# Second attention: the bias is added on VectorE in the instruction that takes the minimum

## The chip, the cores and the metric

One core of a Trainium2 chip. The metric is the device time of one execution in microseconds (us).

## The reference

Two blocks run one after the other on 512 tokens of width 2048, in float32. The first is an S5 layer and a gated attention with 16 heads of 128. The second, which matters here, projects its input to an attention part and to an RWKV-7 part, and puts both through one output matrix. Its attention has 16 heads of 64 channels and mixes three dilated windows by the softmax of their log sums:

```
for window, dilation in DIL_PATTERNS:          # (128, 1), (512, 4), (2048, 16)
    o, lse = dilated_window_attention(q, k, v, dilation, window // dilation)
    ...
wts = jax.nn.softmax(jnp.stack(lses), axis=0)
o = jnp.einsum('pbsh,pbshc->bshc', wts, jnp.stack(outs))
```

This equals one softmax over all keys with the logarithm of a count added to each score: the count says how many of the three patterns hold this query and key (no pattern: minus 1e30). The kernel computes it so. Its table `bias` is minus that logarithm. The scores on chip are negated too, so a row's minimum is what the softmax takes off, and the exponential has scale -1.

## The kernel before

Activations lie with channels on the 128 partitions and the 512 tokens along the free axis. A projection is a chain of output tiles of 128 channels. Each weight tile is loaded by SyncE into `wraw`, split into a high part by ScalarE (`make_hi`) and a low part by GpSimd (`make_lo`), and multiplied with three matmuls for each block of 128 input channels (lines 183 to 185). The order on each engine is the order of the code; semaphores tie the engines together.

The second attention comes after the RWKV part of the second block. Two heads make a pair, for they share one tile of 128 channels; there are 8 pairs and 16 heads, written out without a loop. A head has four blocks of 128 queries, b = 3, 2, 1, 0, and a block has (b + 1) * 128 keys, so 512, 384, 256 and 128. For head h the engines do this:

- TensorE, `at_scores`: for each block the product of queries and keys (line 1822), then two more products with the identity that add the table's high and low part (lines 1823 and 1824, "bias products"). Then the 10 transposes of the probabilities of the head before (`at_transpose`, line 1864). After an even head it transposes the pair's values (`at_turn_v`), after an odd head from 3 on it multiplies the probabilities of pair (h - 3) / 2 with the values (`at_values`, line 1897).
- VectorE: ahead of an even head from 4 on `at_gate` (line 1918, the product with the gate); then the four minima (`at_minima`, line 1834), one of the four copies of the transposed probabilities of the head before (`at_copy_dve`, line 1879), and `at_divide`: a reciprocal of two row sums (line 1852) and two products (line 1855), twice.
- ScalarE: the four exponentials with their row sums (`at_exp`, line 1845), the other three copies (`at_copy_act`, line 1888), and the copy of the values after an even head. After an odd head it rounds one output tile to its high part (line 1625).
- GpSimd: for each pair the sum that finishes the rotation of queries and keys (`at_turn`, line 1804), and between two of these the low part of one output tile (`w2_lo`, line 1630).
- SyncE: `at_load` brings queries, keys and values of a pair and the swapped parts (lines 1787 and 1791), `at_load_z` its gate (line 1797). Two sets of buffers serve even and odd pairs. The load of the gate of pair p waits until `at_gate` of pair p - 2 has run, and the load of pair p + 1 stands behind it in SyncE's queue.

A head has three banks of PSUM, by its parity: its scores and later the transposes of its probabilities lie there, so head h waits for the copies of head h - 2. The scores of an even head wait for `at_turn` of their pair.

Of the kernel before, what the change touches and what calls it, by code (L numbers as in the profile page):

```python
# [75 lines left out]
def program(nc, a):  # L76
    ctx = ExitStack()
    with ctx:
# [1553 lines left out]
        def rw_act(act, p, nxt):  # L1632
# [49 lines left out]
            if not nxt:  # L1682
                act.wait_ge(gemm, N_B)
                w2_hi(act, range(0, 3))
                make_hi(act, N_B + 1, 1, (N_B + 1) // 2)
                w2_hi(act, range(3, NBK))
                act.activation(idr, ident[:, :], ACT.Copy)
                act.activation(bhi, xt["bias"], ACT.Copy).then_inc(a_bh, 1)
                for i in (1, 2):
                    act.wait_ge(gemm, N_B + i)  # L1690
                    make_hi(act, N_B + 1 + i, (1 + i) % 2, (N_B + 1 + i) // 2)
# [60 lines left out]

        flat = [r[:, 13:KT, :].rearrange("p k t -> p (k t)") for r in (rhi, rlo)]
        bhi, blo, idr = flat[0][:, 0:1280], flat[1][:, 0:1280], flat[0][:, 1280:1280 + P]
        a_bh, a_bl = sem("a_bh"), sem("a_bl")
        at["p2"] = xt["bias"]

# [24 lines left out]
        def at_load(sp, p):  # L1782
            u = p % 2
            if p >= 2:
                sp.wait_ge(a_s, 6 * (p - 1))
# [20 lines left out]
        def at_scores(pe, h):  # L1806

            p, hd, u = h // 2, h % 2, h // 2 % 2
            if hd == 0:
                pe.wait_ge(a_qk, p + 1)  # L1810
            if h == 0:
                pe.wait_ge(a_bl, 1)
            if h == 1:
                pe.wait_ge(rw_cn, 8)
                pe.wait_ge(rw_sd, 8)
            for b in (3, 2, 1, 0):
                bank, o = as_at[b]
# [19 lines left out]
        def at_exp(act, h):  # L1837
            hd = h % 2
            if h >= 2:
                act.wait_ge(a_pt, 3 * h - 3)  # L1840
            for b in (3, 2, 1, 0):
                bank, o = as_at[b]
                n = (b + 1) * P
                act.wait_ge(a_mx, 4 * h + (4 - b if b >= 2 else 4))
                act.activation(at[f"s{hd}"][:, tri[b]:tri[b] + n], ab_[hd][bank][:, o:o + n], ACT.Exp, scale=-1.0,  # L1845
                               bias=stat(hd, 0, b, b + 1), accum_out=stat(hd, 1, b, b + 1)).then_inc(a_e, 1)
# [21 lines left out]
        def at_part(h, kb):  # L1868
            bank, o = ap_at[kb]
            n = (4 - kb) * P  # L1870
            return at[f"p{h % 3}"][:, p_tri[kb]:p_tri[kb] + n], ab_[h % 2][bank][:, o:o + n]

        def at_copy_dve(d, h):
            if h >= 3:
                d.wait_ge(a_o, (h - 3) // 2 + 1)
            if h == 2:
                d.wait_ge(a_bl, 1)
            d.wait_ge(a_pt, 3 * h + 3)
            d.tensor_copy(*at_part(h, 0)).then_inc(a_pd, 1)

        def at_copy_act(act, h):
            if h >= 3:
                act.wait_ge(a_o, (h - 3) // 2 + 1)
            if h == 2:
                act.wait_ge(a_bl, 1)
            for kb, n in ((2, 1), (3, 2), (1, 2)):
# [3 lines left out]
        def at_values(pe, p):  # L1890
# [4 lines left out]
            for kb in range(4):  # L1895
                for hd in range(2):
                    ins = pe.matmul(banks[1][hs_[hd], kb * P:T],  # L1897
                                    at[f"vt{p % 2}"][:, kb * P + hd * CH:kb * P + (hd + 1) * CH],
                                    at[f"p{(2 * p + hd) % 3}"][:, p_tri[kb]:p_tri[kb] + (4 - kb) * P],
                                    start=(kb == 0), stop=(kb == 3))  # L1900
# [617 lines left out]
```

## Time and profile before

| | |
|---|---|
| time, median of 3 runs | 3248.46 us (3246.85 to 3249.99) |
| profiled execution, first to last instruction (its span; the page has no other time for it) | 3251.0 us |
| mean granted TensorE clock | 0.984 |
| TensorE busy | 3085.9 us, 95% |
| VectorE busy | 1359.9 us, 42% |
| ScalarE busy | 1142.8 us, 35% |
| GpSimd busy | 1645.1 us, 51% |

The second attention runs from about 2946 to 3072 us of the span. In the trace TensorE is PE, VectorE is DVE, ScalarE is ACT, GpSimd is POOL, SyncE is SP; "q" behind an engine is its queue, and an arrow points from what is read to what is written. SBUF tiles appear under the buffer in which they lie (`g`, `wk`, `rhi`), PSUM as `bank`.

### The profile page before, as it was taken

What the parts mean: (1) busy time and instruction counts of PE and PEld (TensorE: products, weight loads), DVE (VectorE), ACT (ScalarE), POOL (GpSimd) and SP (SyncE); (2) the same over time, 40 slices, a digit from 0 to 9 for tenths busy, and PEclk for the clock granted to TensorE, in tenths of its full rate; (3) what the DMA queues carried; (4) which work ended last, traced back from release to release, by engine and by line L of the source; (5) the groups of instructions that cost most, each with busy time, mean ns of one, the idle gap of its engine ahead of it and who ended that gap; (6) DMA issues with size and microseconds to landing.
All of it is one profiled execution on the core that took longest, in us unless ns stands there. A gap on an engine that the chain in (4) does not pass through costs nothing.

```text
span 3251.0 us, 53322 instructions
## 1 busy us (share of the span) xinstructions
PE 3085.9 (95%) x21260; PEld 2411.6 (74%) x21260; DVE 1359.9 (42%) x2058; ACT 1142.8 (35%) x1524; POOL 1645.1 (51%) x1331
## 2 busy tenths in 40 slices
PE   5899989999899999999999989999999999999997
PEld 4677778878678888888877857777777777765676
DVE  8789882120332221231231054345345345345512
ACT  4355553233432232332333242233233233244421
POOL 2555554444677777777754434443443444443242
PEclk9999999999999999999999999999999999999998
DMA  4466665232222222222222332222222222224422
GB/s 152 139 183 174 181 194 178 92 142 95 86 72 94 94 87 94 84 97 89 88 81 78 105 123 100 79 89 86 79 96 82 76 101 81 81 78 121 141 104 90
DMA packets 126977, 348.14 MB, mean 107 GB/s; under 512 B 59873, under 2 KB 62945, under 8 KB 96241
## 3 DMA queue, kind: packets, MB, share of 16 engines
q1 hardware_dynamic: 126832, 346.00, 32.3%
q8 instruction: 118, 1.93, 0.3%
q14 instruction: 27, 0.21, 0.0%
HBM read 306.33 MB, written 34.90 MB: 105 GB/s over the span
## 4 chain that ended last, share of the span: by engine, by line
PE 73%; issue 10%; POOL 8%; DVE 5%; ACT 2%; DMA 0%; POOLq 0%; ACTq 0%; SPq 0%; DVEq 0%
PE bank L183 21%; PE bank L184 20%; PE bank L185 20%; POOL wlo L167 7%; PE bank L1822 1%; PE bank L1150 1%; PE bank L1168 1%; PE bank L1504 1%; ACT whi L162 1%; PE bank L1515 1%; PE bank L1823 1%; PE bank L1897 1%; PE bank L1159 1%; PE bank L1483 0%; PE bank L924 0%
## 5 line engine op out<-in xcount | busy, mean ns | idle before, releaser
L167 POOL TENSOR_TENSOR wlo<-wraw,whi 128x512 fp32r<-128x512 f32 (+1 forms) x916 | 1225.0, 1369 | 1335.3 <-ACT whi L162 1335.3
L183 PE MATMUL bank<-rhi,whi 128*128 128x512 f32 x3648 | 1490.5, 409 | 85.6 <-DVE rlo L770 29.3
L184 PE MATMUL bank<-rlo,whi 128*128 128x512 f32 x3648 | 1431.5, 392 | 0.0
L185 PE MATMUL bank<-rhi,wlo 128*128 128x512 f32 x3648 | 1430.5, 392 | 0.0
L183 PEld LDWEIGHTS bank<-rhi,whi 128*128 128x128 f32 x3648 | 690.7, 189 | 285.8 <-issue 67.3
L184 PEld LDWEIGHTS bank<-rlo,whi 128*128 128x128 f32 x3648 | 691.7, 190 | 147.6 <-issue 15.3
L185 PEld LDWEIGHTS bank<-rhi,wlo 128*128 128x128 f32 x3648 | 690.6, 189 | 147.7
L162 ACT ACTIVATE whi<-wraw 128x2048 fp32r<-128x2048 f32 (+2 forms) x232 | 437.9, 1887 | 546.5 <-PE bank L185 345.6
L978 POOL TENSOR_TENSOR wraw<-wraw,vec 128x512 f32<-128x512 f32 x260 | 266.8, 1057 | 0.0
L882 DVE TENSOR_TENSOR ssum<-ssum,wk 128x512 f32<-128x512 f32 x30 | 21.6, 718 | 315.5 <-ACT wk L872 315.5
L872 ACT ACTIVATE wk<-bank 128x512 f32<-128x512 f32 x32 | 27.9, 872 | 240.2 <-PE bank L185 240.2
L1723 POOL TENSOR_TENSOR g<-g,wk 128x256 f32<-128x256 f32 x80 | 58.7, 756 | 95.1 <-PE bank L1504 64.7
L1388 DVE TENSOR_TENSOR g<-g,bank 128x512 f32<-128x512 f32 x40 | 27.6, 689 | 157.6 <-PE bank L1515 157.6
L1049 DVE SCALAR_TENSOR_TENSOR wk<-bank,rstd 128x512 f32<-128x512 f32 x16 | 11.1, 692 | 180.5 <-PE bank L185 180.5
L1054 DVE TENSOR_TENSOR wk<-bank,rstd 128x512 f32<-128x512 f32 x16 | 11.1, 692 | 168.7 <-PE bank L185 168.7
L1065 ACT ACTIVATE wk<-wk 128x128 f32<-128x128 f32 (+1 forms) x64 | 35.2, 551 | 107.5 <-DVE wk L1026 107.5
L1079 ACT ACTIVATE wk<-bank 128x512 f32<-128x512 f32 (+1 forms) x64 | 22.8, 442 | 130.9 <-PE bank L1159 130.9
L859 DVE TENSOR_TENSOR wk<-wk,g 128x512 f32<-128x512 f32 x16 | 11.1, 692 | 136.5 <-ACT wk L855 136.5
L1047 DVE TENSOR_TENSOR wk<-bank,rstd 128x512 f32<-128x512 f32 x16 | 11.1, 691 | 135.8 <-PE bank L185 135.8
L1021 DVE TENSOR_TENSOR wk<-wk 128x128 f32<-128x128 f32 x64 | 62.5, 1035 | 0.5
L2025 DVE TENSOR_TENSOR g<-g,bank 128x512 f32 (+1 forms) x16 | 11.0, 688 | 121.0 <-PE bank L185 118.6
L1845 ACT ACTIVATE g<-bank,wk 128x512 f32<-128x512 f32 (+1 forms) x64 | 33.4, 525 | 61.0 <-DVE wk L1834 61.0
(364 smaller groups left out, 3015.2 us busy)
## 6 DMA issues: line engine op xcount, KB each, us to landing
wraw<-in_wall_dram SPq DMA_DIRECT2D x224, 1024.0 KB, 4.9
g<-in_bmat_dram SPq DMA_DIRECT2D x16, 512.0 KB, 4.0
g<-scr_e SPq DMA_DIRECT2D x128, 64.0 KB, 3.2
scr_a<-ssum SPq DMA_DIRECT2D x24, 256.0 KB, 2.1
g<-in_xp_dram SPq DMA_DIRECT2D x4, 1024.0 KB, 11.5
g<-in_cmat_dram SPq DMA_DIRECT2D x16, 256.0 KB, 7.1
scr_u<-wk SPq DMA_DIRECT2D x16, 256.0 KB, 2.4
scr_y<-wk SPq DMA_DIRECT2D x16, 256.0 KB, 3.1
```

The lines of the kernel that those rows point to most:

```text
L162: act.activation(whi[:, slot, c], wraw[:, slot, c], ACT.Copy).then_inc(w_hi, 1)
L167: ins = pool.tensor_tensor(wlo[:, slot, c], wraw[:, slot, c], whi[:, slot, c].bitcast(F32), ALU.subtract)
L183: pe.matmul(acc[slot][:, :], whk, rhi[:, k, :], start=(k == first), stop=False)
L184: pe.matmul(acc[slot][:, :], whk, rlo[:, k, :], start=False, stop=False)
L185: ins = pe.matmul(acc[slot][:, :], wlk, rhi[:, k, :], start=False, stop=(k == last))
L978: ins = pool.tensor_tensor(raw[:, k, :], raw[:, k, :], bc(g, 2, [P, KT // QUARTERS, P]), ALU.mult)
L1021: ins = d.tensor_tensor(dg, dg, mask, ALU.add)
L1065: ins = act.activation(sc, sc, ACT.Exp, bias=mf["nm"][:, b:b + 1], accum_out=mf["sum"][:, b:b + 1])
L1150: ins = pe.matmul(banks[bank][:, at:at + w_], mf["qh"][:, b * P:(b + 1) * P], mf["kh"][:, 0:w_], start=True, stop=True)
L1159: ins = pe.transpose(banks[bank][:, at + (qb - kb) * P:at + (qb - kb + 1) * P], mf["s"][:, tri[qb] + kb * P:tri[qb] + (kb + 1) * P], ident ...
L1723: pool.tensor_tensor(ml[hd].rearrange("p (b t) -> p b t", b=NB), ab4[hd][:, :, 0], bc(lv, 1, [P, NB, CH]), ALU.mult).then_inc(rw_ml, 1)
L1845: act.activation(at[f"s{hd}"][:, tri[b]:tri[b] + n], ab_[hd][bank][:, o:o + n], ACT.Exp, scale=-1.0, bias=stat(hd, 0, b, b + 1), accum_out ...
```

## The change

The bias products go, and with them the preparation of the table's two parts: two copies on ScalarE and a subtraction on GpSimd ahead of the stage. The minimum of a block becomes one instruction, `tensor_tensor_reduce`, that reads the scores in PSUM and the table in SBUF, writes their sum to the SBUF buffer of the head's probabilities and its minimum to the statistics. The exponential then reads that SBUF buffer in place of PSUM. Each of the four blocks now signals by itself (`a_s` counts four in a head, not three). The table stays in SBUF throughout; before, its place was taken over by the third of three buffers for transposed probabilities (`p2`), which now lies in two free pieces of SBUF.

```diff
@@ at_scores
-            if h == 0:
-                pe.wait_ge(a_bl, 1)
...
-                pe.matmul(to, at_q[u][hs_[hd], b * P:(b + 1) * P], at_k[u][hs_[hd], 0:n], start=True, stop=False)
-                pe.matmul(to, idr, bhi[:, tri[b]:tri[b] + n], start=False, stop=False)
-                ins = pe.matmul(to, idr, blo[:, tri[b]:tri[b] + n], start=False, stop=True)
-                if b != 1:
-                    ins.then_inc(a_s, 1)
+                pe.matmul(to, at_q[u][hs_[hd], b * P:(b + 1) * P], at_k[u][hs_[hd], 0:n], start=True, stop=True)\
+                  .then_inc(a_s, 1)
@@ at_minima, at_exp
-            for b in (3, 2, 1, 0):
-                bank, o = as_at[b]
-                d.wait_ge(a_s, 3 * h + min(4 - b, 3))
-                d.tensor_reduce(stat(hd, 0, b, b + 1), ab_[hd][bank][:, o:o + (b + 1) * P], AX.X, ALU.min)\
-                 .then_inc(a_mx, 1)
...
+                d.wait_ge(a_pt, 3 * h - 3)
...
+                d.wait_ge(a_s, 4 * h + (4 - b if b >= 2 else 4))
+                d.tensor_tensor_reduce(at[f"s{hd}"][:, tri[b]:tri[b] + n], ab_[hd][bank][:, o:o + n],
+                                       xt["bias"][:, tri[b]:tri[b] + n], 1.0, 3.0e38, ALU.add, ALU.min,
+                                       stat(hd, 0, b, b + 1)).then_inc(a_mx, 1)
...
-                act.activation(at[f"s{hd}"][:, tri[b]:tri[b] + n], ab_[hd][bank][:, o:o + n], ACT.Exp, scale=-1.0,
+                sc = at[f"s{hd}"][:, tri[b]:tri[b] + (b + 1) * P]
+                act.wait_ge(a_mx, 4 * h + 4 - b)
+                act.activation(sc, sc, ACT.Exp, scale=-1.0,
                                bias=stat(hd, 0, b, b + 1), accum_out=stat(hd, 1, b, b + 1)).then_inc(a_e, 1)
@@ at_part
-            return at[f"p{h % 3}"][:, p_tri[kb]:p_tri[kb] + n], ab_[h % 2][bank][:, o:o + n]
+            return at_p(h, kb), ab_[h % 2][bank][:, o:o + (4 - kb) * P]
...
+            if h % 3 == 2:
+                return p2[0] if kb == 0 else p2[1][:, p_tri[kb] - T:p_tri[kb] - T + n]
+            return at[f"p{h % 3}"][:, p_tri[kb]:p_tri[kb] + n]
@@ rw_act, at_pool
-                act.activation(idr, ident[:, :], ACT.Copy)
-                act.activation(bhi, xt["bias"], ACT.Copy).then_inc(a_bh, 1)
...
-            pool.wait_ge(a_bh, 1)
-            pool.tensor_tensor(blo, xt["bias"], bhi.bitcast(F32), ALU.subtract).then_inc(a_bl, 1)
```

On VectorE, at an even head of the middle of the stage, the rows before the change are these (`a_s` is the semaphore of finished scores, `a_pt` of transposes, `a_e` of exponentials):

```order
L1918 TENSOR_TENSOR g<-bank,g 128x512 [waits a_lz1,a_o]
L1834 TENSOR_REDUCE wk<-bank 128x1 [waits a_s] x4
L1879 COPY wk<-bank 128x512 [waits a_pt,a_o]
L1852 RECIPROCAL wk<-wk 128x2 [waits a_e]
L1855 TENSOR_SCALAR g<-g,wk 128x512 [waits vch]
L1855 TENSOR_SCALAR g<-g,wk 128x384
```

and these with the change, at the same place:

```order
L1910 TENSOR_TENSOR g<-bank,g 128x512 [waits a_lz1,a_o]
L1827 ISA g,wk<-bank,wk 128x512 [waits a_s,a_pt]
L1827 ISA wk 128x1
L1827 ISA g,wk<-bank,wk 128x384 [waits a_s]
L1827 ISA wk 128x1
L1827 ISA g,wk<-bank,wk 128x256 [waits a_s]
L1827 ISA wk 128x1
L1827 ISA g,wk<-bank,wk 128x128 [waits a_s]
L1827 ISA wk 128x1
L1873 COPY wk<-bank 128x512 [waits a_pt,a_o]
L1843 RECIPROCAL wk<-wk 128x2 [waits a_e]
```

Four instructions have become eight: behind each one that adds and reduces stands a second that writes one column, the minimum. The order of all else is kept.

On TensorE, at the scores of an odd head, a piece of the difference:

```order
-L1822 MATMUL bank<-wk 128x512
-L1823 MATMUL bank<-rhi 128x512
-L1824 MATMUL bank<-rlo,rhi 128x512
-L1822 MATMUL bank<-wk 128x384
-L1823 MATMUL bank<-rhi 128x384
-L1824 MATMUL bank<-rlo,rhi 128x384
```

and what stands there with the change:

```order
+L1815 MATMUL bank<-wk 128x512
+L1815 MATMUL bank<-wk 128x384
+L1815 MATMUL bank<-wk 128x256
+L1815 MATMUL bank<-wk 128x128
```

Nothing lies between the products of two blocks any more; transposes and value products follow as before.

## Rows read from the trace of the kernel before

**Rows 1.** The page of the profile, its first line

```profile
span 3251.0 us, 53322 instructions
```

**Rows 2.** Busy time by engine in one stretch of the second attention, then clock, DMA share, GB/s

```profile
2960.00:3063.00 103.00, 100.32 (x484) 56.03 (x483) 63.56 (x153) 50.48 (x161) 26.92 (x18) 1.00 0.35 98
```

**Rows 3.** The chain that ended last, five of its pieces (start us, us, what)

```profile
3004.51 1.05 PE bank L1822 x2
...
3016.40 1.12 PE bank L1864 x10
...
3017.52 2.30 PE bank L1897 x16
...
3019.82 1.05 PE bank L1822 x2
...
3065.76 0.43 PE bank L183
```

**Rows 4.** Timeline of head 7 (start us, us, engine, line), TensorE and one VectorE row

```profile
2997.09 0.55 DVE L1855 TENSOR_SCALAR g<-g,wk 128x256 f32<-128x256 f32 x2
...
2997.14 0.50 PE L1823 MATMUL bank<-rhi 128*128 128x512 f32 x1
...
2997.80 0.91 PE L1822 MATMUL bank<-g 64*128 64x384 f32 x2
...
3000.65 0.33 PE L1823 MATMUL bank<-rhi 128*128 128x128 f32 x1
...
3000.93 1.28 PE L1864 MATMUL bank<-ident,g 128*128 128x128 f32 x10
```

**Rows 5.** VectorE groups by form (count | busy us, mean ns | idle before)

```profile
L1834 DVE TENSOR_REDUCE wk<-bank 128x1 f32<-128x512 f32 x16 | 11.1, 691 | 3.6 <-PE bank L1824 3.2
...
L1016 DVE SCALAR_TENSOR_TENSOR wk<-bank,wk 128x512 f32<-128x512 f32 x16 | 11.9, 742 | 0.0
...
L1016 DVE SCALAR_TENSOR_TENSOR wk<-bank,wk 128x128 f32<-128x128 f32 x16 | 5.6, 351 | 27.6 <-PE bank L1150 27.6
...
L1852 DVE RECIPROCAL wk<-wk 128x2 f32<-128x2 f32 x32 | 5.0, 157 | 0.4 <-ACT g L1845 0.4
...
L428 DVE TENSOR_TENSOR_SCAN bank<-g,bank 128x256 f32<-128x256 f32 x16 | 11.1, 695 | 0.6
```

**Rows 6.** Timeline from the end of head 7 on: one pass of the load of a pair

```profile
2998.94 2.00 POOL L1804 TENSOR_TENSOR wk<-wk 128x1024 f32<-128x1024 f32 x1 [8.74 <-DMA wk<-scr_a]
...
3002.25 0.36 ACT L1845 ACTIVATE g<-bank,wk 128x128 f32<-128x128 f32 x1
...
3003.11 0.82 DVE L1855 TENSOR_SCALAR g<-g,wk 128x512 f32<-128x512 f32 x2
...
3004.04 1.56 DVE L1855 TENSOR_SCALAR g<-g,wk 128x256 f32<-128x256 f32 x2
...
3004.12 1.40 POOL L1630 TENSOR_TENSOR rlo<-g,rhi 128x512 fp32r<-128x512 f32 x1 [3.19 <-ACT rhi L1625]
...
3005.52 0.68 DVE L1918 TENSOR_TENSOR g<-bank,g 128x512 f32<-128x512 f32 x1
...
3006.22 0.35 SPq L1797 DMA_DIRECT2D g<-scr_az  x1
...
3006.67 0.39 SPq L1787 DMA_DIRECT2D g<-scr_a  x1
...
3014.09 2.36 POOL L1804 TENSOR_TENSOR g<-g 128x1024 f32<-128x1024 f32 x1 [8.58 <-DMA g<-scr_a]
```

**Rows 7.** ScalarE, one group by form in the second attention

```profile
L1888 ACT ACTIVATE wk<-bank 128x256 f32<-128x256 f32 x10 | 3.8, 382 | 0.0
```

**Rows 8.** Timeline: first minimum of the stage, and SyncE behind the gates of pairs 0 and 5

```profile
2950.87 1.68 DVE L1834 TENSOR_REDUCE wk<-bank 128x1 f32<-128x512 f32 x4
...
2974.65 0.35 SPq L1797 DMA_DIRECT2D g<-scr_az  x1
...
3051.99 0.35 SPq L1797 DMA_DIRECT2D g<-scr_az  x1
```

More of the change, by code:

```diff
@@ L1751, in program @@
                "in1": g2[:, 0:3 * T], "sw1": g2[:, 3 * T:5 * T]}
[L1753 to L1756, printed above, removed]
+        p2 = [w["u"][:, 0:T], wk[:, 5706:5706 + 768]]
         def at_out(p):
@@ L1784, in at_load @@
             if p >= 2:
-                sp.wait_ge(a_s, 6 * (p - 1))
+                sp.wait_ge(a_s, 8 * (p - 1))
                 sp.wait_ge(a_vt, p - 1)
@@ L1821, in at_scores @@
                 to = ab_[hd][bank][:, o:o + n]
-                pe.matmul(to, at_q[u][hs_[hd], b * P:(b + 1) * P], at_k[u][hs_[hd], 0:n], start=True, stop=False)
-                pe.matmul(to, idr, bhi[:, tri[b]:tri[b] + n], start=False, stop=False)
-                ins = pe.matmul(to, idr, blo[:, tri[b]:tri[b] + n], start=False, stop=True)
-                if b != 1:
-                    ins.then_inc(a_s, 1)
+                pe.matmul(to, at_q[u][hs_[hd], b * P:(b + 1) * P], at_k[u][hs_[hd], 0:n], start=True, stop=True)\
+                  .then_inc(a_s, 1)
         def at_minima(d, h):
             hd = h % 2
-            for b in (3, 2, 1, 0):
-                bank, o = as_at[b]
-                d.wait_ge(a_s, 3 * h + min(4 - b, 3))
-                d.tensor_reduce(stat(hd, 0, b, b + 1), ab_[hd][bank][:, o:o + (b + 1) * P], AX.X, ALU.min)\
-                 .then_inc(a_mx, 1)
-        def at_exp(act, h):
-            hd = h % 2
             if h >= 2:
-                act.wait_ge(a_pt, 3 * h - 3)
+                d.wait_ge(a_pt, 3 * h - 3)
             for b in (3, 2, 1, 0):
@@ L1843, in at_exp @@
                 n = (b + 1) * P
-                act.wait_ge(a_mx, 4 * h + (4 - b if b >= 2 else 4))
-                act.activation(at[f"s{hd}"][:, tri[b]:tri[b] + n], ab_[hd][bank][:, o:o + n], ACT.Exp, scale=-1.0,
+                d.wait_ge(a_s, 4 * h + (4 - b if b >= 2 else 4))
+                d.tensor_tensor_reduce(at[f"s{hd}"][:, tri[b]:tri[b] + n], ab_[hd][bank][:, o:o + n],
+                                       xt["bias"][:, tri[b]:tri[b] + n], 1.0, 3.0e38, ALU.add, ALU.min,
+                                       stat(hd, 0, b, b + 1)).then_inc(a_mx, 1)
+        def at_exp(act, h):
+            hd = h % 2
+            for b in (3, 2, 1, 0):
+                sc = at[f"s{hd}"][:, tri[b]:tri[b] + (b + 1) * P]
+                act.wait_ge(a_mx, 4 * h + 4 - b)
+                act.activation(sc, sc, ACT.Exp, scale=-1.0,
                                bias=stat(hd, 0, b, b + 1), accum_out=stat(hd, 1, b, b + 1)).then_inc(a_e, 1)
@@ L1869, in at_part, with at_p @@
             bank, o = ap_at[kb]
+            return at_p(h, kb), ab_[h % 2][bank][:, o:o + (4 - kb) * P]
+        def at_p(h, kb):
             n = (4 - kb) * P
-            return at[f"p{h % 3}"][:, p_tri[kb]:p_tri[kb] + n], ab_[h % 2][bank][:, o:o + n]
+            if h % 3 == 2:
+                return p2[0] if kb == 0 else p2[1][:, p_tri[kb] - T:p_tri[kb] - T + n]
+            return at[f"p{h % 3}"][:, p_tri[kb]:p_tri[kb] + n]
         def at_copy_dve(d, h):
@@ L1875, in at_copy_dve @@
                 d.wait_ge(a_o, (h - 3) // 2 + 1)
-            if h == 2:
-                d.wait_ge(a_bl, 1)
             d.wait_ge(a_pt, 3 * h + 3)
@@ L1883, in at_copy_act @@
                 act.wait_ge(a_o, (h - 3) // 2 + 1)
-            if h == 2:
-                act.wait_ge(a_bl, 1)
             for kb, n in ((2, 1), (3, 2), (1, 2)):
@@ L1898, in at_values @@
                                     at[f"vt{p % 2}"][:, kb * P + hd * CH:kb * P + (hd + 1) * CH],
-                                    at[f"p{(2 * p + hd) % 3}"][:, p_tri[kb]:p_tri[kb] + (4 - kb) * P],
+                                    at_p(2 * p + hd, kb),
                                     start=(kb == 0), stop=(kb == 3))
```

## The prediction

> **What bounds the kernel now.** I read the span first [rows 1]; 3251.0 us is 2.5 us above the median of the runs shown, and since the sum below is a difference inside one trace, I take it off the median. Next come the busy times over the middle of the second attention [rows 2]: TensorE works 100.3 of 103 us at clock 1.00, VectorE 63.6, ScalarE 50.5, GpSimd 26.9. The chain that ended last says the same: a pair's scores start at 3004.51 and the next pair's at 3019.82, so a pair costs 15.31 us, and what lies between is nearly all TensorE [rows 3]. TensorE is the limit today, so what it loses is worth time until the next loop closes. The question is which loop is next and at what length.
>
> **What the change takes from TensorE.** In head 7 the bias products of the widest block lie between 2997.14 and 2997.80, 0.66 us; those of the narrowest between 3000.65 and 3000.93, 0.28 us [rows 4]. The widths go in even steps, so four blocks cost 2 * (0.66 + 0.28) = 1.9 us a head, 3.8 us a pair. TensorE alone would then need 15.3 - 3.8 = 11.5 us a pair, 30 us less over 16 heads. The copies and the subtraction ahead of the stage had no one waiting for them; I count them at nothing. The work that hides them is the last RWKV pair on TensorE. The reciprocal chain on VectorE that lets the first minimum start only at 2950.87 [rows 8] does not depend on them either, so without that cover nothing changes.
>
> **What it adds to VectorE.** No row shows the fused instruction. The nearest is the first attention's, which also reads scores in PSUM and a table in SBUF and writes SBUF: 0.742 us for 512 columns and 0.351 for 128, against 0.691 for today's minimum of 512 [rows 5]. Four blocks: 2 * (0.742 + 0.351) = 2.2 us. The order shows a second instruction behind each; the smallest VectorE row is 0.157 us [rows 5], the lower bound is nothing. I take 0.157, so 2.8 us a head. Upper bound for the main instruction: the scan, 0.695 us for 256 columns where the first attention's form, on the line between its ends, takes 0.48; that is 0.86 ns a column more, 1.1 us for the 1280 columns of a head. A head on VectorE is then 2.8 for the minima, 0.6 for the copy (it takes 0.69, and the next instruction can start a little before its end), and for the divide 0.2 for the first reciprocal, 0.93 from the first two products to the last two, and 0.55 for these [rows 4, 6], about 1.7. Together 5.1 us, and with the gate's 0.68 [rows 6] a pair is 10.9 us. That is below 11.5: by busy time alone VectorE doesn't bind.
>
> **The loop that closes next.** SyncE can't fetch ahead at will: the load of pair p + 1 stands behind the gate's load of pair p, and that waits for `at_gate` of pair p - 2. Rows 6 show one pass. The gate product ends at 3005.52 + 0.68 = 3006.20; the gate's load is issued at 3006.22, the pair's at 3006.67; GpSimd's sum (`at_turn`) starts at 3014.09, so 7.9 us behind the gate's end; it takes 2.36 us, or 2.00 for the other buffers [rows 6], on average 2.2. So 10.1 us behind a gate the next pair's scores can start, and not before. Today that is early: the sum for pair 4 ended at 3000.94 and its scores start at 3004.51 [rows 3, 6], 3.6 us of slack. The slack is less than the 3.8 us that the change takes from a pair, so this load decides.
>
> Where the sum lands matters too. Today it falls on VectorE's minima. Then it would fall on the divide of the odd head, just ahead of the next gate. In rows 6 the last two products of a divide take 1.56 us where a free one has 0.55 [rows 4], and the gate behind them starts at 3005.52, when GpSimd's `w2_lo` (3004.12 + 1.40) ends. So a GpSimd operation holds VectorE's products: 1.0 us here. The Trainium skill says this in "SBUF — State Buffer", section "Who interferes with whom": GpSimd and a VectorE instruction in a two-port mode exclude each other for a whole instruction, while one with a single SBUF input outside of these modes, as the fused one would be, isn't held. By that rule the products would wait for the whole sum and the minima would not; a price list without it gives rival A's time.
>
> With the hold, one pass is: 10.1 from the gate's end to the end of the sum; then the held products, 0.93 + 0.55 = 1.5; `w2_lo` is queued right behind the sum and gets between them, 1.0; the next gate, 0.7; hand-over 0.1. Sum 13.4 us a pair, against 15.3.
>
> **The sum.** Before pair 2's gate load there is a first stretch. It starts with the minimum at 2950.87, bound by VectorE: four heads at 2.8 + 1.7 less about 0.2 of overlap, three copies of 0.6, a gate of 0.7, are 19.7 us, so 2970.6 without any hold. GpSimd works on two weight tiles, one sum and one `w2_lo` in that stretch; laid out in order, these hold the divides for about 4 us, which puts the first gate's end at 2974.6, where it is now (SyncE follows it at 2974.65 [rows 8]). So it gains 0, at best 4. From the gate of pair 0 to that of pair 5 there are five passes: now 3051.99 - 2974.65 = 77.3 us [rows 8], then 5 * 13.4 = 67.0, a gain of 10.3. The last stretch, from the gate of pair 5 to the end of the values of pair 6, is 3065.76 - 3051.99 = 13.8 us now [rows 3, 8]. Then: minima 2.7, the last exponential 0.36 and its hand-over 0.1 [rows 6], the first copy 0.38 [rows 7], scores of head 15 at (1.05 + 3000.93 - 2997.14) - 1.9 = 2.95, transposes 1.12, values 2.30 [rows 3, 4]: 10.0 with the hand-overs, a gain of 3.8. Behind that nothing is changed and all of it moves up. Total 10.3 + 3.8 = 14.1 us: 3248.5 - 14.1 = 3234.4, I say 3234.5.
>
> **Rivals.** A, no hold: VectorE has finished the divide ahead of the sum, or the products don't wait. Then the load loop is 10.1 + 0.7 + 0.2 = 11.0 us and TensorE's 11.5 decides: 5 * (15.5 - 11.5) = 20, and 3.8, and up to 4 in the first stretch: 3221 to 3225. For it: today's sums cost almost nothing. Against it: 1.56 against 0.55 in rows 6. A 0.14.
>
> B, the fused instruction runs at the scan's pace, 1.1 us a head more. VectorE's pair is 10.9 + 2.2 + 1.0 of hold = 14.1, and waits for TensorE come on top; it saves about 6 us: 3242. For it: both keep a running result. Against it: today's minimum keeps one too at 0.691. "Vector Engine (DVE) Microarchitecture Reference" of the Trainium skill, section "Points that are easy to get wrong", halves such instructions when both sources lie in SBUF and aren't bf16; here one is PSUM, so by its letter it wouldn't, but if it did, this rival is what it gives, 3242. B 0.15.
>
> C, slower: the fused instruction and its second one cost over (15.3 - 0.7 - 1.0) / 2 - 2.3 = 4.5 us a head; from there VectorE alone makes a pair longer than 15.3. At twice the scan's excess they cost 5.0 and the stage grows by 8 pairs * 1.0: 3256. An instruction that no row shows leaves room for it. C 0.08.
>
> The forecast, 3229 to 3239, has 0.58; 0.05 is left for effects outside of the stage. TensorE will wait some 2 us in a pair; the clock is 1.00 in rows 2 and might fall at times, but TensorE's own work isn't what ends last then.
>
> **Numbers.** 0.2% is 6.5 us, about what a measurement of this kernel can tell from no change, so the line is at 3242. Faster: forecast, A, half of B, some of the rest, 0.82. Same 0.10, slower 0.08. The range reaches to A's upper part and to B: 3223 to 3243; the likeliest case alone 3229 to 3239.
>
> **What would show it.** Right: the period of pairs is 13.4 us, TensorE waits for GpSimd's sum at even heads, VectorE's products stretch to 2 us beside it. Fused rows near 0.74 and a small second row. The first gate ends at about 2974.6. Wrong: waits on ScalarE or VectorE in place of the sum, a period of 11.5 (A) or 14 (B), or the fused row above 1.2 us.

## The result, and the profile after

The changed kernel takes 3231.28 us, the median of nine runs (3228.34 to 3241.19), against 3248.46 (nine runs, 3235.61 to 3259.39): the ratio is 0.995, with a 95% interval of 0.9938 to 0.9963, so 12 to 20 us less. The forecast was 3234.5, in a range of 3223 to 3243.

The page of the changed kernel, its first line and the busy times (answers [rows 1]):

```profile
span 3239.4 us, 53124 instructions
...
PE 3062.8 (95%) x21132; PEld 2407.9 (74%) x21132; DVE 1350.7 (42%) x2122; ACT 1141.0 (35%) x1522; POOL 1639.7 (51%) x1330
```

The span is 11.6 us shorter than before. This execution was the longest of its nine (3241.19 us), so it is no measure of the whole gain. What repeats is the stage itself. Below, the **stage** runs from the start of the first minimum to the start of the last gate product (pair 7), and a **pass** from the start of one gate product to the next, for the five passes between the gates of pairs 0 and 5. The stage took 121.3 us before and takes 110.1 now, 11.2 less, while the rest of the span is the same to 0.4 us.

Busy time by engine (TensorE, its weight loads, VectorE, ScalarE, GpSimd), then clock, DMA share and GB/s, in the first stretch (to the gate of pair 0) and in the five passes, for the changed kernel:

```profile
2950.43:2975.51 25.08, 20.93 (x71) 13.44 (x70) 15.40 (x60) 15.72 (x46) 8.99 (x8) 0.59 0.34 97
...
2975.51:3040.98 65.47, 56.80 (x286) 36.91 (x287) 49.84 (x156) 36.28 (x120) 17.57 (x10) 0.92 0.43 121
```

and for the kernel before, cut at the same events:

```profile
2950.87:2973.93 23.06, 21.77 (x105) 12.25 (x105) 15.47 (x44) 15.20 (x46) 9.05 (x8) 1.00 0.37 106
...
2973.93:3051.29 77.36, 75.45 (x362) 41.53 (x362) 48.63 (x117) 36.91 (x120) 17.87 (x10) 1.00 0.37 103
```

The first stretch is 2.0 us longer, at a granted clock of 0.59 in place of 1.00. The passes have gone from 77.4 to 65.5 us at clock 0.92. The last stretch, from the gate of pair 5 to that of pair 7, has gone from 20.9 to 19.6 us, at clock 0.83. TensorE is busy 87% of the passes (56.8 of 65.5), before 98%; VectorE 76%, before 63%. Nothing in the row of the passes is full, so waits set part of the pace.

VectorE by form in the changed kernel's second attention (count | busy us, mean ns | idle before), which answers [rows 5]:

```profile
L1846 DVE TENSOR_SCALAR g<-g,wk 128x512 f32<-128x512 f32 x16 | 13.0, 810 | 0.6
...
L1827 DVE CUSTOM_DVE_ANT_0 g<-bank,wk 128x512 f32<-128x512 f32 x16 | 11.0, 687 | 9.0 <-PE bank L1815 9.0
...
L1827 DVE DVE_READ_ACCUMULATOR2_ANT wk<- 128x1 f32 x64 | 5.3, 83 | 0.0
...
L1827 DVE CUSTOM_DVE_ANT_0 g<-bank,wk 128x128 f32<-128x128 f32 x16 | 4.6, 286 | 0.0
```

The fused instruction is the `CUSTOM_DVE_ANT_0`: 687 ns at 512 columns, 286 at 128 (forecast 742 and 351). The instruction behind it, which writes the minimum, takes 83 ns, not 157. The widest product of the divide shows 810 ns, where it had 499 before.

The chain that ended last, six of its pieces in one pass (start us, us, what), answers [rows 3]:

```profile
2976.23 0.35 SPq L1792
...
2978.57 5.45 DMA g<-scr_a
...
2984.09 2.37 POOL g L1799
...
2986.51 1.78 PE bank L1815 x4
...
2988.45 0.28 DVE g L1846
...
2988.73 0.60 DVE g L1910
```

This is the loop of the forecast: gate, load, sum on GpSimd, scores of an even head, held products, gate. (The chain names the scores because VectorE's queue waits for them next; what the gate itself stands behind are the held products.) The same pass in the timeline (start us, us, engine, line), beside a free pair of products for comparison, answers [rows 6]:

```profile
2984.09 2.36 POOL L1799 TENSOR_TENSOR g<-g 128x1024 f32<-128x1024 f32 x1 [12.79 <-DMA g<-scr_a]
...
2984.57 3.51 DVE L1846 TENSOR_SCALAR g<-g,wk 128x512 f32<-128x512 f32 x2
...
2986.41 1.45 POOL L1630 TENSOR_TENSOR rlo<-g,rhi 128x512 fp32r<-128x512 f32 x1
...
2988.65 0.68 DVE L1910 TENSOR_TENSOR g<-bank,g 128x512 f32<-128x512 f32 x1
...
2989.36 0.35 SPq L1792 DMA_DIRECT2D g<-scr_az  x1
...
3009.80 0.81 DVE L1846 TENSOR_SCALAR g<-g,wk 128x512 f32<-128x512 f32 x2
```

From the gate's load (2976.23) to the sum are 7.86 us, forecast 7.9. The sum lasts 2.36. The two products that start beside it take 3.51 us together, where a free pair takes 0.81, and end only behind `w2_lo`. The next gate comes 2.20 us behind the sum's end (forecast 1.5 + 1.0), and the next gate's load at 2989.36, 13.13 us after the last one.

Not every pass is like this one. The windows of this pass and of the fourth:

```profile
2975.51:2988.65 13.14, 12.09 (x63) 7.68 (x64) 11.20 (x32) 7.19 (x24) 3.77 (x2) 1.00 0.41 120
...
3011.24:3027.60 16.36, 13.31 (x57) 8.84 (x58) 9.01 (x33) 7.50 (x24) 5.55 (x3) 0.79 0.33 96
```

The granted clock of the five passes is 1.00, 0.87, 1.00, 0.79 and 1.00. The first and the last, 13.1 and 13.4 us, have the full clock, and in both TensorE waits for the sum and the products are held. They show the loop of the forecast without the clock in it.

### The profile page after: what moved, and what is told of

It reads as the page before. It is cut to its first block, busy times and chain, and to the rows that moved or that the text cites. A ratio compares the mean times of both kernels' runs of the same rounds, so it can differ in the third digit from the quotient of the medians.

```text
span 3239.4 us, 53124 instructions
## 1 busy us (share of the span) xinstructions
PE 3062.8 (95%) x21132; PEld 2407.9 (74%) x21132; DVE 1350.7 (42%) x2122; ACT 1141.0 (35%) x1522; POOL 1639.7 (51%) x1330
## 4 chain that ended last, share of the span: by engine, by line
PE 73%; issue 9%; DVE 7%; POOL 7%; ACT 2%; DMA 1%; SPq 1%; DVEq 0%; POOLq 0%; ACTq 0%
PE bank L183 21%; PE bank L185 20%; PE bank L184 20%; POOL wlo L167 6%; PE bank L1150 1%; PE bank L1168 1%; PE bank L1815 1%; PE bank L1504 1%; ACT whi L162 1%; PE bank L1515 1%; DVE bank L403 1%; DMA g<-scr_a 1%; PE bank L1159 1%; PE bank L1483 0%; PE bank L1855 0%
## 5 line engine op out<-in xcount | busy, mean ns | idle before, releaser
L184 PEld LDWEIGHTS bank<-rlo,whi 128*128 128x128 f32 x3648 | 692.0, 190 | 147.7 <-issue 15.1
L859 DVE TENSOR_TENSOR wk<-wk,g 128x512 f32<-128x512 f32 x16 | 11.5, 717 | 137.1 <-ACT wk L855 131.5
L2028 ACT ACTIVATE wk<-g 128x512 f32 (+1 forms) x16 | 10.1, 632 | 123.5 <-DVE g L2015 123.5
## 6 DMA issues: line engine op xcount, KB each, us to landing
g<-in_xp_dram SPq DMA_DIRECT2D x4, 1024.0 KB, 11.8
```

What stands on the lines that cost most here:

```text
L184: pe.matmul(acc[slot][:, :], whk, rlo[:, k, :], start=False, stop=False)
```

## The experiments

Each kernel's time stands beside the kernel before on the same chip. "First" is the first stretch, and the clock column gives its granted clock and that of the passes.

| kernel | median us (runs); before | ratio, 95% interval | stage | first | the five passes | clock |
|---|---|---|---|---|---|---|
| before | 3248.46 (9) | | 121.3 | 23.1 | 16.3 15.3 15.3 15.3 15.2 | 1.00, 1.00 |
| changed | 3231.28 (9); 3248.46 | 0.9950, 0.9938 to 0.9963 | 110.1 | 25.1 | 13.1 12.7 9.9 16.4 13.4 | 0.59, 0.92 |
| changed, again | 3231.72 (11); 3247.67 | 0.9952, 0.9938 to 0.9965 | 109.5 | 25.1 | 13.1 12.4 10.0 16.2 13.2 | 0.59, 0.92 |
| load ahead | 3225.14 (5); 3253.92 | 0.9913, 0.9897 to 0.9929 | 93.5 | 22.1 | 11.0 11.2 10.5 10.8 11.0 | 0.69, 1.00 |
| load ahead, again | 3219.57 (5); 3247.67 | 0.9917, 0.9899 to 0.9934 | 93.5 | 22.1 | 11.0 11.2 10.6 10.3 11.5 | 0.69, 1.00 |
| low parts late | 3232.59 (6); 3253.92 | 0.9941, 0.9921 to 0.9962 | 108.9 | 22.1 | 10.0 15.0 10.2 16.0 14.8 | 0.69, 0.92 |
| both | 3227.17 (6); 3253.92 | 0.9919, 0.9902 to 0.9937 | 100.3 | 25.1 | 10.5 10.5 11.8 10.2 14.9 | 0.59, 0.97 |
| filled | 3226.21 (5); 3253.92 | 0.9913, 0.9898 to 0.9929 | 103.0 | 22.1 | 13.2 12.7 13.5 12.5 12.6 | 0.69, 1.00 |
| ahead, early fill | 3223.84 (6); 3248.36 | 0.9928, 0.9912 to 0.9943 | 92.5 | 21.2 | 11.5 10.0 11.8 10.2 11.0 | 0.92, 1.00 |
| filled, low parts late | 3231.66 (4); 3248.36 | 0.9944, 0.9924 to 0.9965 | 103.1 | 22.1 | 12.3 11.9 12.4 12.4 15.6 | 0.69, 1.00 |
| idle products | 3248.16 (10); 3248.36 | 1.0005, 0.9991 to 1.0019 | 120.9 | 22.7 | 16.2 15.3 15.3 15.3 15.1 | 1.00, 1.00 |
| before, load ahead | 3249.09 (10); 3248.36 | 1.0004, 0.9991 to 1.0018 | 124.0 | 25.7 | 16.3 15.3 15.3 15.3 15.2 | stage 0.97 |
| filled, low part doubled | 3231.91 (9); 3247.67 | 0.9959, 0.9943 to 0.9975 | 108.7 | 21.7 | 14.6 13.4 14.2 14.0 13.7 | 0.76, 0.93 |
| filled, gate later | 3239.75 (9); 3247.67 | 0.9980, 0.9966 to 0.9995 | 109.8 | 25.8 | 13.8 13.4 14.3 13.6 14.5 | 0.74, 0.94 |

The stage repeats within 0.6 us in the two kernels that were profiled twice; the rest of the span lies anywhere from 3117 to 3130 us, in every kernel. So causes are read from the stage and the passes, and the timed ratio says what is left of them in the end.

**Load ahead** (changed kernel; the load of pair p + 1 no longer stands behind the gate's load of pair p).

```diff
-            for p in range(2, 8):
-                at_load(sp, p)
+            at_load(sp, 2)
+            for p in range(2, 8):
+                if p < 7:
+                    at_load(sp, p + 1)
                 at_load_z(sp, p)
```

> SyncE issues the load of pair p + 1 ahead of the gate's load of pair p, so it no longer waits for a gate. Load theory (load of a pair plus the hold of VectorE make the loop of 13.1 us a pair in the changed kernel): the sum of queries and keys is early again, no even head waits for it, a pair falls to 11.5 us and the time by 5 * 1.6 = 8 us, to about 3223. Clock theory (TensorE at a granted clock of 0.86 is the limit, the load merely arrives in time): no wait on the sum, but a pair stays near 13 us and the time at 3231. VectorE theory (its own work is the limit): also 3231, with VectorE busy without a gap.

> The load-ahead kernel beside the changed one on the same chip. Load theory: 5 to 12 us less than the changed kernel, passes of 11 us and a stage near 94 us, 16 us less than the first profile of the changed kernel. Rival (the first difference came from the chips): the same time as the changed kernel.

A pass goes to 10.9 us on average and the stage to 93.5, 16.6 less than the changed kernel's. In the repeat, on one chip with the changed kernel, the medians are 3219.57 and 3231.72, 12 us apart. TensorE no longer waits for a sum at any even head of the passes, where in the changed kernel it waits 0.54, 3.09 and 0.95 us at three of the five. So the order in SyncE's queue closed the loop. How much of the 11.0 us that the passes lose is the wait itself, and how much the clock, which is 1.00 where it was 0.92, isn't separated; beside the first and the last pass of the changed kernel, which have the full clock too, a pass is 2.1 and 2.3 us shorter. Of the stage's 16.6 us, 3.0 lie in the first stretch, at clock 0.69 in place of 0.59, and other kernels show the same without this edit. In timed difference to the kernel before it is the fastest kernel of the study. This is also the kernel in which the clock is easiest to follow. Its timeline, two rows of TensorE in the first stretch:

```profile
2941.35 2.43 PE L1855 MATMUL bank<-ident,g 128*128 128x128 f32 x10 [2.64 <-DVE g L1846]
...
2945.29 4.60 PE L1815 MATMUL bank<-g 64*128 64x512 f32 x8 [1.51 <-ACT g L1880]
```

and its windows, 8 us from about the second row on and then the five passes:

```profile
2946.00:2954.00 8.00, 8.00 (x24) 5.37 (x23) 3.67 (x15) 5.47 (x15) 4.87 (x4) 0.51 0.12 25
...
2960.19:3014.71 54.52, 50.50 (x280) 32.13 (x279) 49.71 (x157) 35.46 (x120) 16.18 (x9) 1.00 0.49 129
```

TensorE stood still 2.64 us and then 1.51 us for VectorE and ScalarE, the granted clock went to 0.51, which is the lower level (1.2 of 2.4 GHz) nearly throughout, and the scores of one head took 4.60 us where they take 2.42 at the full level. In the passes it is at 1.00 again, with TensorE busy 93%.

**Low parts late** (changed kernel, `w2_lo` behind the last sum, not between two) and **both** (this and the load ahead).

```diff
                 if p >= 2:
-                    w2_lo(pool, range(p + 5, p + 6))
-            w2_lo(pool, range(13, 14))
+                if p == 2:
+                    w2_lo(pool, range(7, 8))
+            w2_lo(pool, range(8, 14))
```

> GpSimd makes the low parts of output tiles 8 to 12 behind the last sum instead of one behind each sum. Load theory with the hold: the second hold of VectorE's products (1.0 to 1.3 us a pair) goes, 5 passes of it: 3225 to 3226. Clock theory and VectorE theory: within 1 us of 3231, unless the six operations at the end delay the last projection, which would show as a wait of TensorE on line 1630.

> Both edits, the load ahead of the gate's load and the low parts behind the last sum. Load theory: as the first alone, 3222 to 3223, since a sum that is early holds nothing that anyone waits for; the low parts then matter little. Clock theory: 3231. VectorE theory: 3225, because the held time of VectorE falls.

The passes of the first scatter between 10.0 and 16.0 us at clock 0.92, and the time, 3232.59, can't be told from the changed kernel's, so the 5 us that the theory with the hold expected aren't there. The second has four passes of 10.8 on average and a last one of 14.9. Neither isolates the hold: the clock moves with the edit, and the operations that were moved come down on the last pass. Hence the next kernels.

**Filled** (changed kernel, with two products of the identity ahead of the scores of each even head from 4 on; the scores overwrite them, and they are meant to fill TensorE's idle time there) and **filled, low parts late** (this edit and the one before; the first edit is shown).

```diff
+            if h % 2 == 0 and h >= 4:
+                pe.wait_ge(a_pa, 3 * h - 5)
+                bank, o = as_at[3]
+                for _ in range(2):
+                    pe.matmul(ab_[hd][bank][:, o:o + T], ident[:, :], xt["bias"][:, 0:T], start=True, stop=True)
```

> The changed kernel with two more products at each even head from 4 on, ahead of the wait for the sum, which the real product overwrites; they fill 2 us in which TensorE waits. Clock theory: the granted clock in the second attention goes from 0.86 to nearly 1.00 and the time falls by 3 to 8 us. Load theory: passes bound by the load stay at 13 us whatever the clock is, so the time stays within 2 us of 3231, or grows by up to 2 us where the products outlast the wait.

> The low parts of tiles 8 to 12 behind the last sum, together with the two filling products ahead of the wait for each sum from head 4 on. With the fillers alone five passes took 12.9 us each. Hold theory: without the second hold a pass falls by 1.0 to 1.3 us, to about 11.8, and the stage from 103 to 97 us. Rival (that hold is hidden behind something else): passes of 12.9 us again, stage 103 us.

Windows of the first of the two, first stretch and passes:

```profile
2945.25:2967.35 22.10, 17.95 (x72) 11.82 (x71) 16.11 (x61) 15.49 (x46) 9.04 (x8) 0.69 0.37 110
...
2967.35:3031.81 64.46, 61.48 (x305) 36.45 (x304) 53.97 (x156) 35.94 (x120) 18.02 (x10) 1.00 0.43 123
```

The clock is 1.00 in all passes, and their mean is 12.9 us with no outlier. Beside the changed kernel the ratio to the kernel before falls from 0.9950 to 0.9913, and the intervals don't touch; of the 7.1 us that the stage is shorter, 3.0 lie in the first stretch, whose work stands ahead of the added products. So filling the waits helps, as the clock theory said, and the passes stay at 13 us, as the load theory said. But the filled kernel is not the load loop at full clock. Two pieces of its chain that ended last, one pass apart, are the added products:

```profile
2978.97 1.92 PE bank L1808 x4
...
2991.40 1.91 PE bank L1808 x4
```

They lie 12.43 us apart, TensorE waits for no sum in these passes, and 1.9 us of each is filling. TensorE's own order, filling included, is the limit here, with VectorE's held products on top. With the low parts late as well, the first four passes average 12.3 in place of 13.0, 0.7 less each, where 1.0 to 1.3 were expected. In the second, third and fourth the sum is over or all but over when the products start, and these take their free time. In the second:

```profile
2993.84 2.00 POOL L1799 TENSOR_TENSOR wk<-wk 128x1024 f32<-128x1024 f32 x1 [9.16 <-DMA wk<-scr_a]
...
2996.29 0.82 DVE L1851 TENSOR_SCALAR g<-g,wk 128x512 f32<-128x512 f32 x2
```

These three passes are 11.9, 12.4 and 12.4 us all the same, and TensorE's added products again follow each other by 12.43 us. So the 0.7 us is what is left above TensorE's limit, not the full price of the hold. The fifth pass is 15.6, and its rows say why:

```profile
3033.56 2.25 DVE L1851 TENSOR_SCALAR g<-g,wk 128x512 f32<-128x512 f32 x2
...
3034.13 5.30 POOL L1630 TENSOR_TENSOR rlo<-g,rhi 128x512 fp32r<-128x512 f32 x4
...
3035.91 2.37 DVE L1851 TENSOR_SCALAR g<-g,wk 128x256 f32<-128x256 f32 x2
```

Four low parts stand in one row on GpSimd, and two pairs of products that take 0.82 and 0.55 us when free take 2.25 and 2.37 beside them. What the edit saves in four passes it returns in the fifth; the stage is 103.1 against 103.0.

**Ahead, early fill** (load ahead, with two such products ahead of head 2's scores and two behind head 1's).

> The load ahead of the gate's load, and four products with the identity at the start of the stage (two behind the scores of head 1, two ahead of those of head 2) into a bank that the value product overwrites. They fill the two waits, 2.6 and 1.5 us, behind which the profile of the load-ahead kernel shows 14 us at a granted clock of about 0.5. Clock theory: no lower clock at the start, the first stretch (first minimum to the first gate) falls from 22.8 us to 18 or 19, and the stage from 93.5 to about 89 us. Rival (VectorE's chain sets the first stretch, the clock costs nothing there): 93 us, the first stretch as before.

Its first stretch:

```profile
2947.83:2968.99 21.16, 18.00 (x79) 9.70 (x78) 18.19 (x60) 15.16 (x46) 9.33 (x8) 0.92 0.63 177
```

The clock is 0.92 where it was 0.69, and the stretch 21.2 us where it was 22.1. VectorE is busy 18.2 of them, 2.1 more than in the load-ahead kernel. The reason is in its rows:

```profile
2959.49 2.85 DVE L1846 TENSOR_SCALAR g<-g,wk 128x512 f32<-128x512 f32 x2
```

With the higher clock head 2 is done earlier, its products fall beside GpSimd's weight tiles and sum, and its two pairs of products take 2.85 and 1.83 us, where the load-ahead kernel's take 0.82 and 0.55. So the clock gave more than 0.9 us, and the hold took the rest back. The forecast of 18 or 19 us left that out. The timed ratio shows nothing of the 0.9 us.

**Idle products** (changed kernel, with TensorE's load put back: two products with the table's copy ahead of each real one, which overwrites them).

```diff
...
+                for _ in range(2):
+                    pe.matmul(to, idr, bhi[:, tri[b]:tri[b] + n], start=True, stop=True)
                 pe.matmul(to, at_q[u][hs_[hd], b * P:(b + 1) * P], at_k[u][hs_[hd], 0:n], start=True, stop=True)\
```

> The changed kernel, but TensorE still runs two products with the identity for each block, as the kernel before, ahead of the real one, which overwrites them (the table's high part is made again for it). It tells what the fused instruction costs while TensorE has its old load. If TensorE alone is the limit then: stage 121 us as before and the time within 3 us of the kernel before. If VectorE's added work or the later minima show: stage 125 us or more.

Its stage:

```profile
2949.34:3070.24 120.90, 119.31 (x574) 66.86 (x574) 76.26 (x250) 63.14 (x194) 27.74 (x19) 1.00 0.33 98
```

TensorE is busy 119.3 of 120.9 us. The fused instruction, its companion and the exponential's new source are all there, and the time is that of the kernel before: 1.0005, with at most 0.2% of doubt. At this pace they cost nothing on the path, and all of the gain comes from TensorE's products.

**Before, load ahead** (the order of loads alone, on the kernel before).

> The kernel before with the load of pair p + 1 ahead of the gate's load of pair p. The sums end 3.6 us ahead of the scores there, so every theory expects the stage at 121.3 us and no change of time. A gain here would mean that the order of the loads helps by itself, and not because the change made the load the limit.

The passes are the same to 0.05 us, and the time can't be told from the kernel before (1.0004). The order is worth 12 us in the changed kernel and nothing that is measured in the old one, where the load had slack. The stage is 2.6 us longer in this profile, all of it in the first stretch:

```profile
2944.56:2970.25 25.69, 24.78 (x105) 14.39 (x106) 15.21 (x44) 15.29 (x46) 9.05 (x8) 0.87 0.39 118
```

The granted clock fell here too: behind a wait of 0.91 us the ten transposes of head 1 took 2.15 us, where the kernel before, with the same wait at the same place, took 1.1. A fall of the clock is thus not peculiar to the changed kernel.

**Filled, low part doubled** (GpSimd does one low part more in each pass from pair 3 on, into a slot that no one reads).

```diff
                 if p >= 2:
+                    if p >= 3:
+                        pool.wait_ge(r_hi, 96 + p + 6)
+                        pool.wait_ge(r_lo, 96 + p + 5)
+                        pool.tensor_tensor(rlo[:, 14, :], w2_of(p + 5), rhi[:, p + 5, :].bitcast(F32), ALU.subtract)
                     w2_lo(pool, range(p + 5, p + 6))
```

> The kernel with the filling products, and on GpSimd the subtraction that makes the low part of tiles 8 to 12 runs twice in a row (the first time into a place that is written again later). That doubles the operation that holds VectorE's products behind each sum. Hold theory: four of the five passes grow by up to 1.3 us, from 12.9 to about 14.0, the stage from 103 to 107 or 108 us. Rival (GpSimd's operation beside the divide costs nothing on the path): passes of 12.9, stage 103 us.

Its second pass in the timeline, GpSimd and the first two products:

```profile
2982.98 1.99 POOL L1799 TENSOR_TENSOR wk<-wk 128x1024 f32<-128x1024 f32 x1 [8.28 <-DMA wk<-scr_a]
...
2984.93 1.27 POOL L1980 TENSOR_TENSOR rlo<-g,rhi 128x512 fp32r<-128x512 f32 x1
...
2985.09 2.73 DVE L1851 TENSOR_SCALAR g<-g,wk 128x512 f32<-128x512 f32 x2
...
2986.15 1.45 POOL L1630 TENSOR_TENSOR rlo<-g,rhi 128x512 fp32r<-128x512 f32 x1
```

An operation of 1.27 us that no one waits for makes a pass 1.1 us longer on average (14.0 against 12.9). It also wears on the clock, 0.93 in the passes, but not in all of them: the first, third and fifth have 1.00, and they are 1.45, 0.66 and 1.04 us longer than the same passes of the filled kernel. In the first the products take 3.18 us where they took 1.54. So the price is the hold's there and not the clock's. The second and fourth, at 0.87 and 0.76, grow by 0.7 and 1.6, with the clock in them.

**Filled, gate later** (the gate product behind the minima of its head, not ahead of them).

```diff
+                at_minima(d, h)
                 if h % 2 == 0 and h >= 4:
                     at_gate(d, h // 2 - 2)
-                at_minima(d, h)
```

> The kernel with the filling products, and VectorE does the gate product behind the four fused minima of the even head in place of ahead of them. Load theory: the gate starts the loop, so each pass grows by what lies ahead of it now, the fused minima with their waits for the scores, 2.2 to 3 us: passes of 15 to 16 us, the stage near 115 us. Rival (the gate's place doesn't matter, TensorE or VectorE's total work sets the pass): stage within 2 us of 103, since VectorE does the same work.

Four rows of its first pass:

```profile
2982.21 2.34 POOL L1799 TENSOR_TENSOR g<-g 128x1024 f32<-128x1024 f32 x1 [13.10 <-DMA g<-scr_a]
...
2984.60 2.42 PE L1820 MATMUL bank<-g 64*128 64x512 f32 x8 [1.34 <-POOL g L1799]
...
2985.87 0.69 DVE L1832 CUSTOM_DVE_ANT_0 g<-bank,wk 128x512 f32<-128x512 f32 x1 [4.45 <-PE bank L1820]
...
2987.62 0.69 DVE L1915 TENSOR_TENSOR g<-bank,g 128x512 f32<-128x512 f32 x1
```

A pass grows by 1.0 us to 13.9, less than expected, and the clock is 0.94 in place of 1.00. This is the direct form of the loop: in four of the five passes TensorE waits for the sum (1.34, 1.60, 0.23 and 1.44 us) in spite of the filling, the fused instruction then waits 3.3 to 4.7 us for the scores, and the gate stands behind the minima. From one gate to the next are 0.69 for the gate, 7.73 to the sum, 2.34 for it, 0.05 to the scores, 1.27 to the first fused instruction and 1.75 to the gate, 13.8 us. The products are held in one pass only (the second, 3.39 us for 0.55). The growth is small because the filled kernel, from which it counts, stood at TensorE's limit and not at the load's.

**Changed, again.**

> The changed kernel once more, unaltered, so that it and the load-ahead kernel are timed on the same chip. Expected 3231 us, ratio 0.995 to the kernel before. Its trace also tells how far the stage varies with the clock from one execution to another: between 103 us (as with the fillers) and 110 us by the clock theory, 110 us again if something else fixes it.

3231.72 us, the stage 109.5: the passes and even their odd pattern, 10.0 and then 16.2, come back.

## Why the prediction was right, point by point

**What bounded it.** TensorE, as said. What the prediction took off it was too little: a head's scores took 1.05 + 3000.93 - 2997.14 = 4.84 us before [rows 3, 4], and take 2.42 at the full clock, so 2.4 a head where the prediction had 1.9. It had counted the bias products alone, by their widest and narrowest. The rest is in the real products: with nothing between them they take 2.4 us, before they took 2.9 (2.94 in the chain). The forecast of the time didn't hang on it, because TensorE's own need was already below the loop's; rival A's did.

**The fused instruction.** Forecast 2.8 us a head. Measured 0.687 + 0.553 + 0.422 + 0.286 + 4 * 0.083 = 2.3. These rows drop rivals B (a rate like the scan's) and C (over 4.5 us a head). The idle products show that the instruction is hidden at TensorE's old pace.

**The load loop.** Forecast 13.4 us a pass; between the gate loads of pairs 2 and 7 there are 65.5 us, so 13.1. Its parts are as forecast: 7.9 and 7.86 from gate to sum, 2.2 and 2.36 for the sum, 2.5 and 2.20 from there to the gate. That it is the cause is shown by the load ahead (a pass of 10.9), by the same order before the change (no effect), and by the first and last pass, 13.1 and 13.4 us at the full clock. Two pieces of the picture are rougher than the forecast made them. The chain runs through the load in three of the five passes, and at three even heads TensorE waits for the sum, once for long:

```profile
3014.29 4.00 PE L1815 MATMUL bank<-g 64*128 64x512 f32 x8 [3.09 <-POOL g L1799]
```

At the other two TensorE's own work ends later than the sum, part of it at the lower clock (0.87 in the second pass). And two passes are 9.9 and 16.4, because the load of pair 5 took 9.9 us from gate to sum (3001.98 to 3011.90) and so its sum fell behind the gate, not ahead of it. What the short pass saves, the long one pays.

**The hold.** Forecast 1.5 and 1.0 us. The timeline shows it (3.51 for 0.81), and one low part more takes 0.7 to 1.5 us a pass at the full clock. One less gives 0.7, no more because TensorE's filled order is the limit then. The Trainium skill states this in "SBUF — State Buffer", section "Who interferes with whom", as an exclusive lock for a whole instruction. By that rule the fused instruction isn't held, and the trace agrees as far as it shows one: in "filled, low parts late" GpSimd's sum starts at 3031.80 and with it a fused instruction of 128 columns, which takes 0.29 us, its usual time.

**The first stretch.** Forecast: no gain, the gate's end at 2974.6. Measured 2.0 us lost: the gate starts 25.1 us behind the first minimum, before 23.1. The prediction had VectorE as the limit, 19.7 us and about 4 us of held divides. Neither is what happened. All four divides of this stretch take their free time, 0.82 and 0.55 us; no product is held. The chain that ended last is TensorE's from the scores of head 2 on, 17.9 us without a gap, of which three pieces:

```profile
2957.62 4.60 PE bank L1815 x8
...
2965.40 4.56 PE bank L1815 x8
...
2972.29 3.20 PE bank L1889 x16
```

At the full clock these take 2.42, 2.42 and 2.30. VectorE is busy 15.4 of the 25.1 us, and the gate that ends the stretch waits 0.91 us for the value products. The prediction saw that the clock "might fall at times" and dismissed it, since TensorE's own work "isn't what ends last then". **That step failed**, and that its number, no gain, came within 2 us is luck: it had put 4 us on a hold that wasn't there and nothing on a clock that was.

Up to this gate four other kernels have the changed kernel's code. In three (low parts late, filled, both of these together) the stretch is 22.1 us at clock 0.69 in place of 0.59, in the fourth (filled, low part doubled) 21.7 at 0.76. So 1.0 to 1.3 us was to be gained, inside the "at best 4", and 3 us went with the lower clock. In the filled kernel the scores, transposes and values of head 3's turn take 2.78, 1.24 and 2.30 us in place of 4.56, 2.33 and 3.20, which is 3.8 us, and 0.9 comes back as a hold: the last wide products take 1.69 us, not 0.82. Whether the table's preparation cost anything can't be read here. The stage starts 0.4 us earlier than before, but its start moves by over 10 us from one profile to another.

**The last stretch.** Forecast 10.0 us from the end of pair 5's gate to the end of the values of pair 6. It took 12.5 (3041.66 to 3054.15). The chain of the changed kernel over TensorE's last part of it:

```profile
3044.92 3.91 PE bank L1815 x8
...
3048.83 2.33 PE bank L1855 x10
...
3051.16 2.99 PE bank L1889 x16
```

and of the filled kernel, where the whole stretch takes 9.4 (3032.49 to 3041.86):

```profile
3035.89 2.42 PE bank L1820 x8
...
3038.31 1.24 PE bank L1860 x10
...
3039.55 2.30 PE bank L1894 x16
```

3.1 us lie between the two stretches, and these three pieces cover it: 1.5 in the scores, 1.1 in the transposes and 0.7 in the values, the same instructions at a lower and at the full clock. The forecast of 10.0 was sound at 1.00. Here too the step that failed is the clock, put at nothing.

**The sum.** Forecast 14.1 us: 0 in the first stretch, 10.3 in the passes, 3.8 behind them. In the profiled execution the stage gained 11.2: -2.0, 11.9 and 1.3. The load loop gave 1.6 more than said and the two ends, where the clock was low, 4.5 less. The filled kernel gains 18.3 (121.3 - 103.0). Of the 7.1 us between the two, 3.0 lie ahead of the first gate, where the code is the same and only the executions differ, and 3.1 behind the passes, where no product is added and the same instructions run at 0.83 and at 1.00. The 1.0 in the passes isn't a price of the clock, for the filled passes carry 1.9 us of filling each.

The timed difference is 17.2 us, 12 to 20. The forecast lies in that interval, the stage's 11.2 just below it. Where the other 6 us are isn't shown; the rest of the span moves by 13 us from one profile to another, and the stage of the kernel before is known from one profile. So the load loop and the fused instruction were forecast rightly, and that the whole sum comes so near is in part luck.

**Rivals.** A gave 3221 to 3225, 23 to 28 us less than the kernel before, for a kernel whose pace TensorE sets, since nothing is held. The load ahead comes near that (28 and 29 us less than the kernel before on its chip; 10.9 us a pass against A's 11.5), but by another road: the products are still held in it, and it is the load that no longer waits. The changed kernel itself is no A: its two full-clock passes with a sum that is waited for have held products and 13.1 and 13.4 us.

**What stays open.** What decides how long the clock stays low in the first stretch: the changed kernel has 0.59 twice and the load ahead 0.69 twice, but "both" has 0.59, and "filled" and "filled, low part doubled" have the changed kernel's code up to there and 0.69 and 0.76. The change does go with a lower clock in this stretch: seven kernels with the new minima and nothing added to TensorE there have 0.59 to 0.76, the idle products 1.00, the kernel before 1.00, and with the load ahead 0.87. Why the load of pair 5 took 9.9 us is open too. And no kernel keeps the changed kernel's work and order at the full clock in all passes.

## What to carry to other kernels

When work is taken off the engine that bounds a stage, walk the next loop through the queues of loads, not only through the busy times: here a load behind another load that waits cost nothing before the change and some 12 us after it. Then ask what the relieved engine's new waits do to its clock: here the last stretch was 3.1 us longer at the lower level, and a forecast that took TensorE off the critical path had put that at nothing. When you fill the waits to test this, look whether the filling has become the limit itself. And an operation on GpSimd that no one waits for still has a price where VectorE's SBUF products run beside it.

## What the runs showed of the hardware

- Adding a second source in SBUF and a write of the whole block to a minimum out of PSUM costs VectorE next to nothing: 687 ns for 512 columns against 691 for the minimum alone, 286 against 281 for 128. What it adds is the second instruction, 83 ns. "VectorE: DVE Perf Modes" of the Trainium skill, section "Two Vector instructions with no wait between them", says that an operation that writes out its accumulator is two instructions; the trace agrees.
- The exponential from SBUF takes 722 ns at 512 columns, from PSUM 688.
- Two VectorE products beside two GpSimd operations are through only when these are: in the pass shown the products end 0.2 us behind GpSimd's second operation, though GpSimd had started 0.48 us ahead of them.
- Two waits of TensorE, 2.64 and 1.51 us, were followed by some 8 us at a granted clock of 0.51, in which it was busy throughout. In the kernel before with the load ahead the clock fell behind a wait of 0.91 us, in the kernel before it stayed at 1.00 behind the same wait.
- The hold depends on where the operations fall: at granted clock 0.59 no product of the first stretch was held, at 0.92 two pairs took 4.7 us instead of 1.4.
